# The weight sums of a seven-product down projection, added by GpSimd in place of VectorE

## The reference

```
u = jnp.square(jax.nn.relu(jnp.einsum('bsd,df->bsf', h, w_up[l])))
x = x + rms_norm(jnp.einsum('bsf,fd->bsd', u, w_down[l]), norm_mlp_post[l])
```

## Time and profile before

| | us |
|---|---|
| time, median of 3 runs (1925.43 to 1925.70) | 1925.51 |
| the profiled execution's own time | 1926.45 |
| its span, first to last instruction | 1923.9 |
| TensorE busy in the span | 1910.9 |
| VectorE busy | 1310.4 |
| ScalarE busy | 982.3 |
| GpSimd busy | 19.8 |

### The profile page before, as it was taken

The page is one execution under the profiler, slowest core; times in us unless marked ns, Lnnn a source line. Parts: engine busy times, 40 slices in busy tenths (PEclk is TensorE's granted clock), DMA queues, the critical chain, the costliest instruction groups (busy, mean ns, idle before and its releaser), DMA issues.

```text
span 1923.9 us, 21889 instructions
## 1 busy us (share of the span) xinstructions
PE 1910.9 (99%) x8722; PEld 1592.1 (83%) x8722; DVE 1310.4 (68%) x1311; ACT 982.3 (51%) x955; POOL 19.8 (1%) x31
## 2 busy tenths in 40 slices
PE   9999999999999999999999999999999999999998
PEld 7888888888888888888888888887889888888886
DVE  7847648854666654444558988898587869676655
ACT  7334435545435444445455555565556446544553
POOL 0000000000000000000000000000000000000000
PEclk9999999999999999999999999999999999999999
DMA  9866977775767378897885473656678554556753
GB/s 323 257 224 177 275 244 226 226 252 192 250 209 271 110 237 250 246 275 239 246 289 189 173 265 137 232 199 218 200 216 261 178 168 155 171 175 226 234 201 110
DMA packets 386853, 419.66 MB, mean 218 GB/s; under 512 B 192700, under 2 KB 205248, under 8 KB 385600
## 3 DMA queue, kind: packets, MB, share of 16 engines
q1 hardware_dynamic: 385736, 416.69, 67.3%
q10 hardware_dynamic: 1016, 1.59, 0.2%
HBM read 390.96 MB, written 27.27 MB: 217 GB/s over the span
## 4 chain that ended last, share of the span: by engine, by line
PE 90%; DVE 5%; ACT 2%; issue 1%; DMA 1%; ACTq 0%; SPq 0%; POOL 0%; POOLq 0%; DVEq 0%
PE acc L1855 85%; PE mis L1855 4%; DVE lo L1184 3%; DVE m L1164 1%; ACT hi L751 1%; DVE at L1230 1%; PE mis L1858 1%; DMA m<-in_w_down 0%; DVE xs L1164 0%; DMA raw<-in_w_down 0%; ACT m L729 0%; ACT hi L748 0%; DVE xs L1172 0%; DVE m L1530 0%; DVE at L1226 0%
## 5 line engine op out<-in xcount | busy, mean ns | idle before, releaser
L1855 PE MATMUL acc<-hi,at 128*128 128x512 f32 (+1 forms) x5184 | 1603.9, 388 | 1.8 <-DVE lo L1184 0.9
L1855 PEld LDWEIGHTS acc<-hi,at 128*128 128x128 f32 x5184 | 969.9, 188 | 196.8 <-issue 1.4
L1855 PE MATMUL acc<-lo,at 128*128 128x512 f32 (+1 forms) x2592 | 1001.4, 387 | 0.0
L1184 DVE TENSOR_TENSOR lo<-raw,hi 128x2048 fp32r<-128x2048 f32 (+1 forms) x313 | 703.1, 2258 | 391.4 <-ACT hi L751 388.9
L751 ACT ACTIVATE hi<-raw 128x2048 fp32r<-128x2048 f32 (+1 forms) x308 | 576.7, 1887 | 282.0 <-PE acc L1855 125.9
L1855 PEld LDWEIGHTS acc<-lo,at 128*128 128x128 f32 x2592 | 486.7, 188 | 95.9 <-DVE lo L1194 0.3
L729 ACT ACTIVATE m<-acc,st 128x512 f32<-128x512 f32 (+2 forms) x104 | 69.7, 670 | 212.4 <-PE acc L1855 211.4
L1164 DVE TENSOR_TENSOR m<-m 128x256 f32<-128x256 f32 (+1 forms) x147 | 76.5, 520 | 28.3 <-ACT m L729 23.8
L729 ACT ACTIVATE m<-m 128x512 f32<-128x512 f32 (+4 forms) x71 | 58.2, 819 | 60.5 <-DVE m L1164 37.9
L790 ACT ACTIVATE at<-m 128x512 fp32r<-128x512 f32 x40 | 25.1, 631 | 75.3 <-DVE m L1164 53.9
L1184 DVE TENSOR_TENSOR lo<-xs,hi 128x2048 fp32r<-128x2048 f32 x22 | 50.3, 2288 | 6.5 <-ACT hi L751 5.2
(11 more groups left out here) (151 smaller groups left out, 779.9 us busy)
## 6 DMA issues: line engine op xcount, KB each, us to landing
raw<-in_w_in SPq DMA_DIRECT2D x133, 1024.0 KB, 5.4
raw<-in_w_up SPq DMA_DIRECT2D x64, 1024.0 KB, 6.8
raw<-in_w_down SPq DMA_DIRECT2D x44, 1024.0 KB, 6.9
raw<-in_w_out SPq DMA_DIRECT2D x32, 1024.0 KB, 5.6
m<-turned SPq DMA_DIRECT2D x144, 128.0 KB, 3.6
raw<-in_w_pg SPq DMA_DIRECT2D x16, 1024.0 KB, 5.6
turned<-m SPq DMA_DIRECT2D x28, 512.0 KB, 7.0
xs<-in_w_down SPq DMA_DIRECT2D x12, 1024.0 KB, 5.9
```

What stands on the lines that cost most here:

```text
L1184: e.tensor_tensor(lo, raw, hi.bitcast(F32), ALU.subtract).then_inc(s_lo.on("lo", n))
L1855: return e.matmul(o, a, b, start=start, stop=stop)
```

## The change

The four additions T1 to T4 of each of the four groups, 16 in all, move from VectorE's queue to GpSimd's. Their operands, order and buffers are the same. GpSimd waits for the same `low` (and the same transfer) as VectorE did; ScalarE's `high` and SyncE's loads wait for GpSimd's semaphore in place of VectorE's.

```diff
@@ def raw(n), on SyncE @@
-                        sp.wait_ge(s_dve, "sum", chunks[past][6][:2], {3: "T3", 5: "T4"}[chunks[past][6][2]])
+                        sp.wait_ge(s_pool, "sum", chunks[past][6][:2], {3: "T3", 5: "T4"}[chunks[past][6][2]])
@@ on GpSimd @@
+            def sums(n):
+
+                p, g, q = chunks[n][6]
+                x, y = SUMS_OF[g], SUMS_OF[1 - g]
+                b22, b21 = (dn_at[p, "AB"[g] + i] for i in "35")
+                name, o, other = {0: ("T1", x, y), 1: ("T2", x, b22), 3: ("T3", y, b22), 5: ("T4", x, b21)}[q]
+                po.wait_ge(s_lo, "lo", n)
+                if q == 0:
+                    po.wait_ge(loaded("b12"), "b12", p, g)
+                if q == 1:
+                    po.wait_ge(s_raw[raw_slot[b22]], "raw", b22)
+                po.wait_ge(s_pool, LAST)
+                e.tensor_tensor(o, o, other if q == 0 else as2(raw_of(other)), ALU.add).then_inc(s_pool.on("sum", (p, g), name))
...
             for n in range(N_ALL):
+                for c in ahead.get(n, ()):
+                    if is_seven(c) and chunks[c][6][2] in (0, 1, 3, 5):
+                        sums(c)
@@ def high(n), on ScalarE @@
-                        ac.wait_ge(s_dve, "sum", (p, g), {1: "T1", 2: "T2", 4: "T3", 6: "T4"}[q])
+                        ac.wait_ge(s_pool, "sum", (p, g), {1: "T1", 2: "T2", 4: "T3", 6: "T4"}[q])
@@ on VectorE @@
-            def sums(n):
-
...
-                if q == 0:
-                    dv.wait_ge(loaded("b12"), "b12", p, g)
-                    tt(x, x, y, ALU.add).then_inc(s_dve.on("sum", (p, g), "T1"))
...
                     elif c not in spare:
                         low(c)
-                        if is_seven(c):
-                            sums(c)
```

## The result

The changed kernel takes 1938.59 us (median of 4 runs, 1938.11 to 1941.69) against 1925.61 for the kernel before: ratio 1.0069, 95% interval 1.0056 to 1.0081, **13.0 us slower**. The forecast was slower, 1940.0. One execution of 11116 us, among the 11 with the first group's sums moved (experiment 4), stands apart, and nothing on record explains it; the median there is the same with or without it.

The account below looks back on a forecast made before the run. TensorE, busy 1910.9 of 1923.9 us, was taken to bound the kernel. Stalls of 9.4 + 0.8 + 6.6 less 0.7, about +16 us on 1925.51, gave 1941.5, put at 1940; range 1924.9 to 1950.

Parts of the forecast that it names:

- TensorE sets the end, nothing to gain: Whole kernel: removing 36.7 us of VectorE work beside TensorE's gains at most 0.7 us.
- The price of a sum: One 2048-column addition on GpSimd takes 4.4 us, the middle of 3.5 and 5.2, against 2.29 on VectorE.
- Exclusion: VectorE's two-SBUF-input instructions and GpSimd's sums block each other for a whole instruction; chance 0.60, range 1931 to 1953 us.
- Who gets in: At each sum's release, GpSimd takes the shared way in right after `cut`, ahead of `form` and `low`.
- the walk: Following the queues through both halves under mutual blocking to find TensorE's stalls: about +16 us.
- 9a: Plain chunk ahead of product B1, second half: T1's late transfer makes B1 late, costing 0.2 us.
- The second half: Late transfer and sums holding up plain chunks behind group B: 9.4 us, and about 0.8 in the tail.
- 9b: Plain chunk after B1, second half: T2 holds up its `form` and `low`, so TensorE waits 4.7 us.
- 10b: Later plain chunk, second half: T3 holds it up the same way, 0.9 us more.
- 12a and tail: End of the second half: T4 stands before 12a's `low`, 3.6 us; tail about 0.8, before subtracting the earlier 0.7.
- The first half: Group B: T1's late transfer delays T2, so 11a waits 5.6 us; T3 before 12a adds 1.0; together 6.6.
- Rival 1: Sums and VectorE run side by side without contention, sums up to 6.3 us stay hidden: 1925.2 us; chance 0.20.

Follow-up runs that it names:

- experiment 4: Changed kernel with only some groups' sums on GpSimd, the rest on VectorE: last group alone 1933.78 us, other three 1931.30, first alone 1926.27.
- experiment 1: Changed kernel with each of the 16 GpSimd additions replaced by three fills of about the same length that read nothing, sums left out: 1930.57 us.
- 2: Kernel before, sums still on VectorE, with two GpSimd additions of 512 columns on constants beside each sum: 1937.48 us.
- experiment 3: Changed kernel with `form` (two inputs) replaced by a one-input transposition, activations' sums and differences left out: 1936.8 us, one run.
- "polite" order: Changed kernel with each sum waiting for the next plain chunk's `low`: 1983.93 us; or with each sum cut into four additions of 512 columns: 1976.71 us.

## Why the prediction was right

- **TensorE sets the end, nothing to gain:** right. In the runs with fills of 1.81 and 3.67 us VectorE was rid of all 16 sums, and the time stayed within 0.2 us of before.
- **The price of a sum,** 4.4 us: 4.5 in the trace. The middle of two readings of the fills (3.5 and 5.2) was a guess, and that it came so near is partly luck. The Trainium skill, "GPSIMD Engine Reference", section "Elementwise — side-by-side cycle accounting", has 4497 ns, and the trace agrees (4.46).
- **Exclusion:** shown, by the stretched `form`, by experiment 1 (nothing read, nothing stretched), by 2 and by 3. It was taken from one row, at 40.08, that may have another cause (the first power of its kind); no run has that power without the `low` beside it, so the row itself stays open, and the forecast was lucky in it. The row at 1691.22, where a `low` ran beside a reading instruction unhindered, still stands against a hold to the end of every instruction; for the long additions the hold is as assumed.
- **Who gets in:** the walk let `cut` go first and the sum next, and so it is with T2. At T1 of group B, second half, GpSimd got in before the `cut` of 9a.
- **The second half,** 9.4 + 0.8 less 0.7 = 9.5 us walked: 11.88 - 2.44 = 9.4 measured. The parts are less exact than their sum. 9a: 2.0 (walked 0.2). 9b: 2.7 of delay (4.7), so that both together fit, 4.7 against 4.9, and only the split is wrong. Then 1.75 of slow clock, which the walk didn't have; 10b: nothing (0.9); 12a and tail: 3.0 (3.6 and 0.1). That the slow clock and the shorter waits behind it all but cancel is luck as far as the forecast goes.
- **The first half** was mis-sized: 6.6 walked, 1.9 measured. The step is T1 of group B, which I let wait for a transfer of 9 us. The transfer was issued at 1071.11 and the sum began at 1077.30, so it had landed in 6.2 us; T2 was recorded from 1087.33 and not from 1092.2, and 11a waited 0.6 us, not 5.6. The 9.00 us were read in the second half, where two other loads were issued just ahead (at 1220.50 and 1220.89, this one at 1221.37); in the first half none was issued in the 5 us ahead of it. That this is the difference is likely, not tested. The walk's 16.1 us were 3.1 too many. Of the 4.8 us that the two halves gave too much, 1.7 are hidden by what no term stands for: 0.58 before any sum, 0.5 behind 15b, and 0.6 between the spans and the medians. That part is luck, and so is the step from 1941.5 down to 1940, for which the forecast had no row.
- **Rival 1** was given a threshold of 6.3 us and a time of 1925.2. The exclusion rules it out, but its price was wrong too: late sums without exclusion cost 4.2 us (experiment 1), which would be about 1929.8. It looked at the margin of one spot; the profile of experiment 1 has its extra waits elsewhere, 0.24 us at 11a and 1.05 at 15b.

What stays open: the 2.6 us between the profile of experiment 1 and its median, with it why three fills cost 4.2 us where two cost nothing, and how the two groups behind the first share the 4.9 us.

## What to carry to other kernels

Moving two-input SBUF work from VectorE to GpSimd does not relieve VectorE when what stays there has two SBUF inputs too: 2.29 us of work became a hold of 4.5 us, and VectorE's busy time rose. It was free here only where VectorE's chain had margin (the first group). A neighbour with one input passes, but the next one with two inputs is held in its place (experiment 3, 1936.8 us). And before work is moved to a slower engine or made to yield, close the loop that it stands in and compare it with the bounding engine's time per turn: past that, a delay of a few us repeats, and a "polite" order cost four times here what the collision did.

## What the runs showed that was not expected

- GpSimd gets the way in between two VectorE instructions even when only about 0.04 us lie between them (the end of `cut` at 1247.23, `form` at 1247.27), and where it is already waiting it comes before the next one (T1 at 1237.08, ahead of the `cut` at 1237.77).
- TensorE's granted clock went to 0.50, the 1.2 GHz level, about 1 us after it had resumed from a wait of 2.55 us, with one of 1.76 some 10 us before; it was back at 1.00 by 1260. In the run with only the last group moved it followed the wait of 3.16 us at 12a (0.83 over 1280 to 1300). In the first case that cost 1.75 us, about a seventh of the whole loss. The wait of 2.14 us at 12a in the changed kernel had no such drop, nor had those of 1.51 and 1.93 us at 9a and 9b in experiment 3.
